# The recurrence's solve with blocks of 32 on four tiles of the array, and semaphores cleared inside the next block

## The reference, cut to what matters

```python
def step(state, inp):
    r_t, w_t, k_t, v_t, kk_t, a_t = inp
    sa = jnp.einsum('bhvk,bhk->bhv', state, -kk_t)
    state = (state * w_t[:, :, None, :]
             + sa[..., :, None] * (kk_t * a_t)[..., None, :]
             + v_t[..., :, None] * k_t[..., None, :])
    out = jnp.einsum('bhvk,bhk->bhv', state, r_t)
    return state, out
_, out = lax.scan(step, state0, xs, reverse=reverse)
```

## Time and profile before

| | us |
|---|---|
| three runs | 3098.47, 3103.48, 3103.51 |
| median | 3103.48 |
| the profiled execution's own time | 3100.74 |
| its span (first to last instruction) | 3099.0 |
| the 8 solves and what stands between them | from 180.5 to 386 |

### The profile page before, as it was taken

The page is one execution under the profiler, slowest core; times in us unless marked ns, Lnnn a source line. Parts: engine busy times, 40 slices in busy tenths (PEclk is TensorE's granted clock), DMA queues, the critical chain, the costliest instruction groups (busy, mean ns, idle before and its releaser), DMA issues. The chain is left out here.

```text
span 3099.0 us, 55557 instructions
## 1 busy us (share of the span) xinstructions
PE 3003.1 (97%) x20135; PEld 2648.1 (85%) x20135; DVE 2218.0 (72%) x3931; ACT 965.5 (31%) x1789; POOL 1137.1 (37%) x808
## 2 busy tenths in 40 slices
PE   8999989899999999999999999999999999899999
PEld 6678868799999999999999997768888878588887
DVE  7766687788898898688888886577775345577741
ACT  2444421333434334333333333461211023321110
POOL 5244335222222122144333334214555443245553
PEclk9999999999999999999999999999999999899999
DMA  4100023377878877899999963112223241122333
GB/s 163 34 3 3 3 82 107 118 236 255 297 248 264 287 248 268 289 378 359 349 354 339 352 216 100 38 48 94 96 95 95 79 99 35 55 89 95 99 91 94
DMA packets 241745, 507.91 MB, mean 164 GB/s; under 512 B 44534, under 2 KB 135814, under 8 KB 238124
## 3 DMA queue, kind: packets, MB, share of 16 engines
q1 hardware_dynamic: 182828, 321.11, 31.2%
q0 software_dynamic: 36864, 134.23, 13.3%
q10 hardware_dynamic: 21888, 50.34, 4.2%
HBM read 453.17 MB, written 52.44 MB: 163 GB/s over the span
## 5 line engine op out<-in xcount | busy, mean ns | idle before, releaser
L198 POOL TENSOR_TENSOR up_low<-normed,up_high 128x1024 fp32r<-128x1024 f32 (+1 forms) x136 | 317.2, 2332 | 300.6 <-DVE up_high L193 300.6
L3039 POOL DMA_INDIRECT ev_rows<-in_v,ev_list x128 | 180.1, 1407 | 321.1 <-DVE ev_row_sum L3106 307.7
L203 PE MATMUL up_ps<-ffn_high,up_high 128*128 128x512 f32 x704 | 274.9, 390 | 3.0 <-DVEq L828 3.0
L205 PE MATMUL up_ps<-ffn_high,up_low 128*128 128x512 f32 x704 | 273.9, 389 | 0.0
L204 PE MATMUL up_ps<-ffn_low,up_high 128*128 128x512 f32 x704 | 273.9, 389 | 0.0
L203 PE MATMUL eu_ps<-norm_unit_high,expert_high 128*128 128x384 f32 x768 | 265.4, 346 | 0.0
L205 PE MATMUL eu_ps<-norm_unit_high,expert_low 128*128 128x384 f32 x768 | 257.9, 336 | 0.0
L204 PE MATMUL eu_ps<-norm_unit_low,expert_high 128*128 128x384 f32 x768 | 257.7, 336 | 0.0
L193 DVE CAST up_high<-normed 128x1024 fp32r<-128x1024 f32 (+1 forms) x136 | 91.7, 675 | 206.2 <-PE up_down_ps L205 150.6
L2716 POOL DMA_INDIRECT expert_scores<-in_u,eu_list x64 | 84.2, 1316 | 268.5 <-DVE eu_dots L2744 260.2
L3064 ACT ACTIVATE expert_high<-mixed 128x1024 fp32r<-128x1024 f32 x95 | 100.8, 1061 | 228.9 <-PE ev_acc L205 208.7
(11 more groups left out here) (709 smaller groups left out, 8615.5 us busy)
## 6 DMA issues: line engine op xcount, KB each, us to landing
mixed<-in_v SPq DMA_DIRECT2D x128, 512.0 KB
normed<-in_u SPq DMA_DIRECT2D x125, 512.0 KB
normed<-in_w_up SPq DMA_DIRECT2D x88, 512.0 KB, 3.4
expert_act<-mixed ACTq DMA_DIRECT2D x128, 192.0 KB
expert_gates<-eu_gates ACTq DMA_DIRECT2D x24, 1024.0 KB
expert_scores<-expert_gates SPq DMA_DIRECT2D x16, 1536.0 KB
normed<-expert_act SPq DMA_DIRECT2D x128, 192.0 KB
normed<-in_w_down SPq DMA_DIRECT2D x32, 448.0 KB, 3.3
```

The lines of the kernel that those rows point to most:

```text
L198: return nc.gpsimd.tensor_tensor(low.bitcast(F32R), of, high, ALU.subtract)
L203: nc.tensor.matmul(out, w_high.bitcast(F32R), x_high.bitcast(F32R), start=start, stop=False)
L205: return nc.tensor.matmul(out, w_low.bitcast(F32R), x_high.bitcast(F32R), start=False, stop=stop)
L3039: nc.gpsimd.indirect_dma_start(rows[:, b % 4, :], None, v, bass.IndirectOffsetOnAxis(ap=list_[:, b % 8:b % 8 + 1], axis=0)).then_inc(fetch ...
```

## The change

Three things change. The diagonal blocks to invert become 32 wide, four in a unit, one for each quarter of the partitions (`quarter`). So `LEVELS` is 5, that is 4 levels. Step E has 32 matmuls of 32 rows, 32 columns and 32 moving columns, step T has 32 of 32 rows, 32 columns and 64 moving columns, each matmul in the tile of its own quarter. The inverses of 32 are then joined to inverses of 64: G turns one diagonal inverse and multiplies the block between the two by the other (32 small matmuls in two groups), V multiplies these results (16 small matmuls in two groups), and ACT and DVE each copy their half of every result. Masks for the quarters are made by POOL before the recurrence (4 copies and 4 memsets more). DVE's `z` moves from level 4 to behind the copies of C. And `clear_semaphores` is split: `retire_semaphores` only notes which semaphores are done with, and POOL clears them as its first act in the next block, with no second barrier. There is a fifth such place, behind the first feed-forward part, which clears nothing before.

```diff
-def clear_semaphores(nc, c):
-
-    nc.clear_and_free_semaphores(c.taken)
-    nc.all_engine_barrier()
-    c.taken, c.apart = c.apart, []
+def retire_semaphores(c):
+
+    assert not c.stale
+    c.stale, c.taken, c.apart = c.taken, c.apart, []
+
+
+def clear_stale(nc, c):
+
+
+    nc.clear_and_free_semaphores(c.stale)
+    c.stale = []
...
             @block.gpsimd
             def _(pool):
+                clear_stale(nc, c)
                 following.begin_low(pool)
...
-LEVELS = 6
+LEVELS = 5
+QUARTER = 32
...
-        if at == (4, 0):
+        if at == "z":
...
     ACT, solve:
-                            act_s[d].ends(nc.scalar.activation(square[:, of_group(i), 0:HEAD], e_bank[i][:, 0:2, 0:HEAD], ACT.Copy), f"E{n}{i}")
+                            act_s[d].ends(nc.scalar.activation(square[:, of_group(i), 0:QUARTER], e_bank[i][:, 0:2, 0:QUARTER], ACT.Copy), f"E{n}{i}")
...
+                    r = quarter[near[d]]
+                    for g in range(2):
+                        pe_s[d].wait(act, m, f"G{g}")
+                        nc.scalar.activation(square[r, of_join(g), 0:QUARTER], join(turn_bank[g])[r, :, :], ACT.Copy)
+                        act_s[d].ends(nc.scalar.activation(square[r, of_join(g), QUARTER:HEAD], join(join_bank[g])[r, :, :], ACT.Copy), f"G{g}")
+                    for g in range(2):
+                        pe_s[d].wait(act, m, f"V{g}")
+                        act_s[d].ends(nc.scalar.activation(inverse_t[r, of_join(g), quarter[far[d]]], join(joined_bank[g])[r, :, :], ACT.Copy), f"V{g}")
...
     DVE, solve (and the same copies for the other half):
                         done.ends(nc.vector.tensor_copy(square[mine, ST * h:ST * h + ST, HEAD:P], c_bank[h][mine, :, 0:HEAD]), f"C{h}")
+                    beside("z")
...
     PE, solve:
-                                for x in half:
-                                    ins = nc.tensor.matmul(e_bank[i][x, k, 0:HEAD], inverse_t[x, u, :], pw[x, u, 0:HEAD], start=True, stop=True)
+                                for q_, x in enumerate(quarter):
+                                    ins = nc.tensor.matmul(e_bank[i][x, k, 0:QUARTER], inverse_t[x, u, own(q_)], pw[x, u, own(q_)], start=True, stop=True)
...
-                                for x in half:
-                                    ins = nc.tensor.matmul(t_bank[i][x, k, 0:HEAD], square[x, u, 0:HEAD], inverse_t[x, u, :], start=True, stop=True)
+                                for x in quarter:
+                                    ins = nc.tensor.matmul(t_bank[i][x, k, 0:HEAD], square[x, u, 0:QUARTER], inverse_t[x, u, :], start=True, stop=True)
...
+                    for g in range(2):
+                        dve_s[d].wait(pe, m, f"T{LEVELS - 1}{2 * g + 1}")
+                        for k in range(ST):
+                            u = ST * g + k
+                            for x in range(2):
+                                here, there = quarter[2 * x + a_], quarter[2 * x + b_]
+                                nc.tensor.matmul(join(turn_bank[g])[here, k, :], inverse_t[here, u, quarter[a_]], unit[here, quarter[a_]], start=True, stop=True)
+                                ins = nc.tensor.matmul(join(join_bank[g])[here, k, :], pw[there, u, quarter[a_]], inverse_t[there, u, quarter[b_]], start=True, stop=True)
+                        pe_s[d].ends(ins, f"G{g}")
+                    for g in range(2):
+                        act_s[d].wait(pe, m, f"G{g}")
+                        dve_s[d].wait(pe, m, f"G{g}")
+                        for k in range(ST):
+                            u = ST * g + k
+                            for x in range(2):
+                                here = quarter[2 * x + a_]
+                                ins = nc.tensor.matmul(join(joined_bank[g])[here, k, :], square[here, u, 0:QUARTER], square[here, u, QUARTER:HEAD], start=True, stop=True)
+                        pe_s[d].ends(ins, f"V{g}")
                     one, two_ = first_half[d], second_half[d]
                     for h in range(2):
-                        dve_s[d].wait(pe, m, f"T{LEVELS - 1}{2 * h + 1}")
+                        act_s[d].wait(pe, m, f"V{h}")
+                        dve_s[d].wait(pe, m, f"V{h}")
```

More of the change, by code:

```diff
@@ L87, in __init__ @@
     def __init__(self):
-        self.taken, self.apart = [], []
+        self.taken, self.apart, self.stale = [], [], []
     def semaphore(self, nc, name):
@@ L1142, in __init__ @@
         pe_names = [["tr_z", "tr_b", "tr_k"] + (["tr_v"] if d == 0 else []) + tail for d in range(2)]
-        dve_names = ["g", "z"] + mats + [x for x in levels if x[0] == "T"] + ["C0", "C1", "X0", "X1"]
+        dve_names = ["g", "z"] + mats + [x for x in levels if x[0] == "T"] + joined + ["C0", "C1", "X0", "X1"]
         for n in range(ST):
             dve_names += [f"sa{n}"] + ([] if n else ["z_t"]) + ([f"decayed{n}", f"state{n}"] if n < ST - 1 else [])
-        tail = ["low0", "low1", "U"] + [x for x in levels if x[0] == "E"] + ["Y0", "Y1"] + ["out%d" % n for n in range(ST)]
+        tail = ["low0", "low1", "U"] + [x for x in levels if x[0] == "E"] + joined + ["Y0", "Y1"] + ["out%d" % n for n in range(ST)]
         act_names = [["eq", "ek", "ez", "f", "zn", "bn", "kn"] + (["vn"] if d == 0 else []) + tail for d in range(2)]
@@ L1162, in constants @@
         made = 3
-        for own, of_ in ((self.upper, c.upper), (self.lower, c.lower), (self.unit, c.ident)):
+        for own, of_ in ((self.upper, c.upper), (self.lower, c.lower), (self.unit, c.ident),
+                         (self.upper_quarters, c.upper), (self.lower_quarters, c.lower)):
             for x in (slice(0, HEAD), slice(HEAD, P)):
@@ L1166, in constants @@
                 nc.gpsimd.tensor_copy(own[x, :], of_[x, x]).then_inc(self.made, 1)
+                made += 1
+        for own, side in ((self.upper_quarters, 0), (self.lower_quarters, 1)):
+            for x in range(2):
+                pool.wait_ge(self.made, made)
+                first = x * HEAD + side * QUARTER
+                nc.gpsimd.memset(own[first:first + QUARTER, (1 - side) * QUARTER:(2 - side) * QUARTER], 0.0).then_inc(self.made, 1)
                 made += 1
@@ L1697, in mixer_scan @@
         of_group = lambda i: slice(2 * i, 2 * i + 2)
+        quarter = [slice(QUARTER * n, QUARTER * n + QUARTER) for n in range(4)]
+        own = lambda n: quarter[n % 2]
+        near, far = (0, 1), (1, 0)
+        turn_bank, join_bank, joined_bank = (ps[4], ps[3]), (ps[5], ps[1]), (ps[6], ps[7])
+        of_join = lambda g: slice(ST * g, ST * g + ST)
+        join = lambda bank: bank[:, :, :].rearrange("p a n -> p (a n)")[:, 0:P].rearrange("p (u n) -> p u n", n=QUARTER)
         def mask_of(d, kind):
             first, other, with_self = (c.upper, lower, c.upper_eq) if d == 0 else (c.lower, upper, c.lower_eq)
-            return {"Lt": upper if d == 0 else lower, "L": other, "zk": first, "qb": with_self, "qk": with_self}[kind][:, :].unsqueeze(1)
+            return {"Lt": ahead.upper_quarters if d == 0 else ahead.lower_quarters, "L": other, "zk": first, "qb": with_self, "qk": with_self}[kind][:, :].unsqueeze(1)
         with nc.Block() as block:
@@ L1805, in solve @@
                                 beside((n, i // 2))
+                    r = quarter[2 + near[d]]
+                    for g in range(2):
+                        pe_s[d].wait(dve, m, f"G{g}")
+                        nc.vector.tensor_copy(square[r, of_join(g), 0:QUARTER], join(turn_bank[g])[r, :, :])
+                        done.ends(nc.vector.tensor_copy(square[r, of_join(g), QUARTER:HEAD], join(join_bank[g])[r, :, :]), f"G{g}")
+                    for g in range(2):
+                        pe_s[d].wait(dve, m, f"V{g}")
+                        done.ends(nc.vector.tensor_copy(inverse_t[r, of_join(g), quarter[far[d]]], join(joined_bank[g])[r, :, :]), f"V{g}")
                     for h in range(2):
@@ L4429, in build @@
                     if layer == 0:
+                        taken, c.taken = c.taken, []
                         after = LateNorm(nc, c, "attn1", c.y[:, 0:2, :], c.y[:, 2, :], c.y[:, 3, :], c.y[:, 9, :], before=late)
                         stream = gla_stream(nc, c, a, places(c.h, 2 * PLACE, 3) + places(c.y, 5 * S, 1))
+                        c.apart, c.taken = c.taken, taken
                         feed_forward(nc, c, f"up{layer}", weights, down, late, f"conv{layer}", ff_high, ff_low, after=after, following=stream, ahead=4)
                         late = after
+                        retire_semaphores(c)
                     else:
```

20 lines of the change are left out of this document (14 added, 6 removed).

## The result

| | before | after |
|---|---|---|
| median of the runs | 3103.49 us (3098.47 to 3103.70, 4 runs) | 3161.22 us (3158.82 to 3162.49, 4 runs) |
| profiled span | 3099.0 us | 3157.1 us |
| ratio | | 1.0187, 95% interval 1.0176 to 1.0199 |

The changed kernel is slower by 57.7 us; 11.9 us less had been forecast. The page first: busy time, the clock in 40 slices, and the queue that brings instructions.

What follows compares the result with a forecast made beforehand. PE's issue was taken to bound a plain level at 1.86 us. Seven solves 1.04 us shorter and one 0.68 (8.0 us), plus 3.9 us from semaphores, made 11.9 us less: 3091.6 us, range 3086 to 3100.

Steps and rivals of the forecast that it cites:

- the first rival: In the solve, 32-column records cost what 64-column ones do (issue at 14.2 ns, or instruction fetch); 3099.6 us; chance 0.20.
- A lower clock is none: A lower clock was dismissed as a rival: the steps keep 1.00 with PE busy 6.28 of 7.90 us.
- the record of 32 columns on four tiles: In the new step E, a small record takes 8.5 ns, bounds 7.1 and 14.2 ns.
- the second rival: Four row tiles in one bank run slower in the solve, T at 29 ns a record; 3125 us; chance 0.08.
- The first T: In a plain solve, T1 starts 0.87 us after E1, whatever E takes.
- The third rival: PE needs 28.4 ns to start a 32-column record, so both steps take 1.82 us; 3157 us; chance 0.02.
- the join: In each solve, joining inverses of 32 to 64: 2.94 us from the last T's start to C.
- The plain level of 1.66 us: In the solve, the chain of results bounds a level at 1.66 us against 1.86 before.
- The barriers: At four places, second barriers go: 4.5 us of ACT waits, 3.9 us net, bounds 2.5 and 4.5.
- the 0.6 us given back for the clears on POOL: Clears hold up POOL's first work in the next block: 0.2 us at the third place, 0.4 at the fourth.
- The fourth rival: The barriers' gain doesn't come, as POOL or first loads end the next block's wait anyway; 3094.6 us; chance 0.04.
- my 0.36 us for what it gives: Moving `z` out of the solve's levels cuts preparation from 0.81 to 0.45 us a solve, bounds 0.2 and 0.81.

Runs made afterwards that it cites:

- e4: Changed kernel, but steps E and T of its four levels on two 64-wide tiles as before; 3097.94 us, ratio 0.9984.
- e8: Changed kernel, but only one of eight products of a step computed from the second level on; output not the reference's; 3103.61 us.
- e3: Kernel before, each product of step E made in two halves of 32 moving columns; 3138.49 us.
- e9: e8 with 64-wide products added beside the 32-wide ones of each step from the second level on; 3189.14 us.
- e12: Kernel before, 64-wide tiles, products of every second chunk left out from the second level on; output not the reference's; 3095.69 us.
- e13: Kernel before, 64-wide tiles, only one of four products a step from the second level on; output not the reference's; 3111.84 us.
- e6: Kernel before, products of steps E and T made a second time on the idle quadrants from the second level on; 3149.12 us.
- e1: Kernel before with only the semaphores' edit, second barriers gone and clears moved into the next block; 3095.84 us, ratio 0.9982.

## Why the prediction was wrong

**The step that failed** is in the first rival: "twice as many need one every 2.7 us, which still fits". Two errors are in it. The 1.17 us of the earlier trace rows is how long a packet's transfer keeps the queue, and I took it for the time in which the next 256 instructions can be had; the runs show 3.5 to 4.0 us from one restart to the next. (Half of 5.6 us is 2.8 and not 2.7, which changes nothing.) And 39 packets in 220 us is an average over solves and steps. Inside the solves of before the packets start 4.0 to 4.6 us apart (178.28, 182.89, 186.90, 191.19), already near the limit. In the changed kernel's solve, at 132 instructions a microsecond, they are due every 1.9 us. The Trainium skill, Runtime: NRT & Kernel Launch, Instruction fetch mechanics, says that instructions are refilled in blocks of 256 while the current ones run, and that crossing a block's end is mostly hidden. The blocks of 256 are in the trace; the crossing is hidden in the solves of up to 67 a microsecond, and costs PE 1.0 to 2.3 us at a time in those of the changed kernel.

**The second failed step**: "A lower clock is none". I looked at the steps, where PE keeps 1.00, and not at what the new solve would ask of the array: blocks of 32 in place of blocks of 64. The clock was 0.50 from 190.80 to 200.40, which is 1.2 of 2.4 GHz: it fell after almost 10 us of small products and idle stretches, and came back some 2.8 us behind the solve's end. The seven stretches of steps and the one behind the last C have 17.3 us more. Both errors point to the same habit: costing the changed stage record by record, and its supply and clock from averages over before.

**Right**: the record of 32 columns on four tiles. E's 64 loads take 0.69 us with a tail of 0.11, 9.2 ns a record (forecast 8.5, bounds 7.1 and 14.2); so the first rival's other half, issue at 14.2 ns, didn't occur. T takes 0.93 us with its tail on four row tiles in one bank, 13 ns a record (14.2), so the second rival, a shared bank, didn't either. The first T comes 0.88 us behind E (0.87). The third rival gave 3157 us, close to the measured time, but by records at 28.4 ns that no row shows; its number is an accident. The least gap of about 25 ns between starts that the Trainium skill, TensorE: Matmul & The Clock Gate, gives in its part on the gap of 56 ns was weighed in the prediction; the same rows don't agree with it, 9.2 ns over four tiles.

**Mis-sized**: the join, 3.57 us from the last T to C in e4 against 2.94 (3.51 in the last solve, with nothing beside it). The plain level of 1.66 us can't be read in the changed kernel, since every level from the second on has a stall in it or next to it; E to E is 1.75 us in the first. Even with instructions for free the gain was small: e8's solves, with the clock as it was, are 0.35 to 1.35 us shorter than before's, and its steps and the stretch behind the last C lose 18.1 us against 7.5 won. The barriers gave 5.3 to 7.1 us in the times (ratios 0.9982, 0.9983 and 0.9977, with intervals from 2.5 to 9.9 us) where 3.9 stood, with a bound of 4.5. The traces say which part was wrong: 4.7 us of waits went, so the 0.6 us given back for the clears on POOL wasn't due, and the 3.1 us of lower clock behind two of the barriers stood nowhere in the sum. It is the second failed step once more. The fourth rival, no gain from the barriers, is out. `z` was worth 0.03 us a solve. Its 0.68 us on DVE stood in a level in which PE's issue was the bound, so my 0.36 us for what it gives was wrong for levels of 1.86 us; for shorter levels it was not tried.

**What stays open**: why PE goes on only 2.3 to 3.0 us behind the start of a packet that takes 1.0 to 1.5 us, and why the next packet starts only some 1.1 us after that restart. And how much of the 50.6 us in the solves is the clock's: 45.7 us are waits for issue in the levels and the join, but no run had this many 32-wide products at full clock.

## What to carry to other kernels

Count the instructions of a stage and divide by the time that it is to take, before looking at what each costs. Here TensorE was fed 64 to 74 a microsecond when it waited for them, weight loads and matmuls together, so cutting a product into smaller ones on more tiles pays only below that; read the packets of the instruction queue inside the stage, by their starts, not by their busy share over a longer stretch. And look for what the engine's clock does behind a stage that asks less of the array: what is saved in it can be lost, at half the clock, in the work behind it. A barrier can bring the same: what it cost here was its wait and, at two of the four places, another 1.5 to 1.6 us lost to a lower clock behind it.

## What the runs showed of the hardware

- Instructions for TensorE came in packets of 16 KB, 256 of them; where PE waited for them it went on every 3.45 to 4.01 us, and the next packet mostly started about 1.1 us after it had gone on.
- Four 32-wide tiles take a record every 9.2 ns, weights of 32 columns, 32 moving. With 64 weight columns a record cost a tile 58 ns for 32 moving columns as for 64 (e3).
- A change between 32-wide and 64-wide products cost about 0.12 us each at full clock (e9, an estimate, worked out above from 0.43 us for six loads).
- The clock fell to its lower level in and behind solves with few or small products, also on 64-wide tiles (e12 and e13), while stalls of up to 1.9 us between full 64-wide bursts left it at 1.00 (e6).
- Behind the first two of the second barriers, whose waits cost PE 0.9 to 1.5 us each, the clock of before was at its lower level for some 3 us (0.54 and 0.50); without them, at 1.00 (e1).
